# Rotated queries and retention keys turned by VectorE in squares of 32 and by DMAs, in place of TensorE transposes

## What is computed

```python
for l in range(DEPTH_2):
    h = rms_norm(x, pre_norm_g[l])
    (rq, rk, rv, rg, dq, dk, dv, dg, lx, lg) = jnp.split(jnp.einsum('bsd,de->bse', h, w_in[l]), split_idx, axis=-1)
    ro = retention(rq, rk, rv, positions)             # 6 heads of 128, rotated q and k, decayed causal scores
    do = diff_attention(dq, dk, dv, positions, lam)   # 4 heads, 2 x 64 rotated q and k, two softmaxes
    ... # lru_out from lx, lg
    y = jnp.einsum('bse,ed->bsd', mixed, w_out[l])
    x = x + rms_norm(y, post_norm_g[l])
```

## Time and profile before

| what | value |
|---|---|
| median of 3 executions | 2645.58 us (2645.3 to 2647.14) |
| profiled execution | 2647.02 us, span 2645.2 us |
| PE busy | 2556.9 us, 97% |
| PEld busy | 2147.6 us, 81% |
| DVE busy | 1699.3 us, 64% |
| ACT busy | 1282.6 us, 48% |
| POOL busy | 63.3 us, 2% |
| mean granted TensorE clock | 0.994 of full |
| DMA queue of SP (q1), share of 16 engines | 64.6% |

### The profile page before, as it was taken

The page is one execution under the profiler, slowest core; times in us unless marked ns, Lnnn a source line. Parts: engine busy times, 40 slices in busy tenths (PEclk is TensorE's granted clock), DMA queues, the critical chain, the costliest instruction groups (busy, mean ns, idle before and its releaser), DMA issues.

```text
span 2645.2 us, 33987 instructions
## 1 busy us (share of the span) xinstructions
PE 2556.9 (97%) x12327; PEld 2147.6 (81%) x12327; DVE 1699.3 (64%) x2194; ACT 1282.6 (48%) x1824; POOL 63.3 (2%) x102
## 2 busy tenths in 40 slices
PE   3889999999999999999999999999999999999999
PEld 3888887888887887788888888888888887988887
DVE  5887776776676755566655545565666655676664
ACT  3345455444555444544443444455755545565553
POOL 0000000000000000000000000000000100010000
PEclk9999999999999999999999999999999999999999
DMA  9984665888675765687756666556665465665564
GB/s 363 340 262 152 184 207 183 286 308 269 205 251 192 237 205 180 192 281 252 269 190 192 191 191 190 183 186 182 182 188 175 136 216 148 187 187 176 150 200 135
DMA packets 279921, 555.73 MB, mean 210 GB/s; under 512 B 24287, under 2 KB 45101, under 8 KB 279117
## 3 DMA queue, kind: packets, MB, share of 16 engines
q1 hardware_dynamic: 274048, 541.79, 64.6%
q0 software_dynamic: 3040, 8.69, 1.0%
q10 hardware_dynamic: 2668, 3.09, 0.3%
HBM read 549.83 MB, written 2.10 MB: 209 GB/s over the span
## 4 chain that ended last, share of the span: by engine, by line
PE 90%; DVE 4%; ACT 2%; issue 1%; DMA 1%; SPq 0%; POOL 0%; DVEq 0%; ACTq 0%
PE gp L830 83%; PE tp L830 5%; PE tp L833 2%; DMA raw_first<-in_ada_w_dram 1%; DVE wlo L1884 1%; ACT whi L1270 1%; DVE acc L1890 1%; DVE xs L1884 0%; ACT hraw L1270 0%; SPq L813 0%; DVE stat L2208 0%; ACT sx L1270 0%; DVE sx L1884 0%; DVE yd L1884 0%; ACT h L1270 0%
## 5 line engine op out<-in xcount | busy, mean ns | idle before, releaser
L1884 DVE TENSOR_TENSOR wlo<-raw,whi 128x1024 fp32r<-128x1024 f32 (+1 forms) x830 | 986.1, 1197 | 699.7 <-ACT whi L1270 697.1
L830 PE MATMUL gp<-whi,h 128*128 128x512 f32 (+1 forms) x4352 | 1373.2, 389 | 11.5 <-DVE h L1884 5.5
L1270 ACT ACTIVATE whi<-raw 128x1024 fp32r<-128x1024 f32 (+1 forms) x830 | 851.5, 1037 | 666.6 <-PE gp L830 537.3
L830 PEld LDWEIGHTS gp<-whi,h 128*128 128x128 f32 x4352 | 816.4, 188 | 171.5 <-issue 19.6
L830 PE MATMUL gp<-wlo,h 128*128 128x512 f32 (+1 forms) x2176 | 835.6, 384 | 0.0
L830 PEld LDWEIGHTS gp<-wlo,h 128*128 128x128 f32 x2176 | 410.4, 189 | 72.8 <-issue 1.7
L1890 DVE SCALAR_TENSOR_TENSOR acc<-raw,cact,acc 128x1024 f32<-128x1024 f32 x149 | 190.6, 1279 | 7.7 <-DMA raw<-in_ada_w_dram 7.0
L830 PE MATMUL gp<-whi,ah 128*128 128x512 f32 x352 | 138.0, 392 | 0.0
L830 PE MATMUL gp<-whi,al 128*128 128x512 f32 x352 | 137.1, 390 | 0.0
L830 PE MATMUL gp<-wlo,ah 128*128 128x512 f32 x352 | 137.0, 389 | 0.0
L830 PE MATMUL gp<-h,whi 128*128 128x256 f32 (+1 forms) x528 | 107.2, 300 | 20.7 <-ACT whi L1270 10.7
(11 more groups left out here) (331 smaller groups left out, 2594.2 us busy)
## 6 DMA issues: line engine op xcount, KB each, us to landing
raw<-in_w_in_dram SPq DMA_DIRECT2D x310, 512.0 KB, 4.3
raw<-in_ffn_w_in_dram SPq DMA_DIRECT2D x176, 512.0 KB, 4.5
raw<-in_ada_w_dram SPq DMA_DIRECT2D x158, 512.0 KB, 5.0
raw<-in_w_out_dram SPq DMA_DIRECT2D x96, 512.0 KB, 4.4
raw<-in_ffn_w_down_dram SPq DMA_DIRECT2D x88, 512.0 KB, 4.4
raw<-in_w_in_dram SPq DMA_DIRECT2D x64, 384.0 KB, 3.5
raw_first<-in_ada_w_dram SPq DMA_DIRECT2D x34, 512.0 KB, 7.5
raw<-in_gla_wo_dram SPq DMA_DIRECT2D x32, 512.0 KB, 5.7
```

The costliest lines, as they stand in the source:

```text
L830: return e.matmul(o, l, r, start=start, stop=stop)
L1270: return e.activation(o, i, f, **kw)
L1884: return e.tensor_tensor(o, a, b, op)
```

## The change

The planner gives dq and rqk, in place of the two steps `rp_T`, one step `rp_t`, the one after the second rotation step (so one unit later), with no PSUM bank. dk keeps its way over PE. `rp_t` on DVE turns each 128 tokens in squares of 32 with one transpose of 128 x 512, from `st` to a new buffer STT, written in steps of four values; before, it waits until the last job's DMAs have landed. `rp_t` on POOL waits for both transposes and issues 16 DMAs inside SBUF, each of 32 partitions x 2 x 512 bytes, that carry the squares to their partitions, into DQB or RQB: four tiles interleaved, so a tile's values stand 16 bytes apart. `df_S` reads its stationary side (the query) so, `rt_S` both sides. PE waits for the DMAs (`d_rp`) where it waited for ACT's copies, and ACT waits for `rp_turned` before it fills `st` again.

```diff
     if kind in ("dq", "dk", "rqk"):
         l, j = args
-        return [step(("rp_r", (kind, l, j, 0), 0), need=[("lru", l)]), step(("rp_r", (kind, l, j, 1), 0)), idle, idle] + \
-            [step(("rp_T", (kind, l, j, k), 1)) for k in (0, 2)] + [idle]
+        steps = [step(("rp_r", (kind, l, j, 0), 0), need=[("lru", l)]), step(("rp_r", (kind, l, j, 1), 0))]
+        if kind == "dk":
+            return steps + [idle, idle] + [step(("rp_T", (kind, l, j, k), 1)) for k in (0, 2)] + [idle]
+        return steps + [step(("rp_t", (kind, l, j), 0))] + [idle] * 4
...
+    STT, DQB, RQB = w2("stt", 0, [2, 512]), w2("dqb", 32, [1, S, 4]), w2("rqb", 56.25, [3, S, 4])
...
+    def quadrants(b, n, t0, t1):
+
+        return b[:, n // 4, P * t0:P * t1, n % 4]
...
         def roped(kind, l, j):
+            if kind != "dk":
+                w.wait_ge(d_rp, at("rp", kind, l, j))
+                return
...
-            mm(bk[:, 0:S], RQK[:, 6 + h, 0:P], RQK[:, h, :], True, True)
-            mm(bk[:, S:384], RQK[:, 6 + h, P:S], RQK[:, h, P:S], True, True).then_inc(tp_full[u.b], 1)
+            first, second = (quadrants(RQB, 6 + h, t, t + 1) for t in range(2))
+            mm(bk[:, 0:S], first, quadrants(RQB, h, 0, 2), True, True)
+            mm(bk[:, S:384], second, quadrants(RQB, h, 1, 2), True, True).then_inc(tp_full[u.b], 1)
...
-                last = mm(bk[:, c0:c0 + n], DQT[rows, h, t * P:(t + 1) * P], DKT[c if h < 2 else 0][rows, h, 0:n], True, True)
+                last = mm(bk[:, c0:c0 + n], quadrants(DQB[rows], h, t, t + 1), DKT[c if h < 2 else 0][rows, h, 0:n], True, True)
...
+                    if of[0] in ("dq", "rqk"):
+                        w.wait_ge(rp_turned, at("turned", *of))
...
+        def rp_t(us, kind, l, j):
+            w.wait_ge(rope_done, at("rope", kind, l, j))
+            w.wait_ge(d_rp, 256 * rp_n[0])
+            rp_n[0] += 1
+            for t in range(2):
+                e.transpose(STT[:, t, :].rearrange("p (q i b) -> p q b i", q=4, b=4),
+                            ST2[job_of[kind, l, j]["st2"]][:, t, :].rearrange("p (b q i) -> p q b i", q=4, b=4)).then_inc(rp_turned, 1)
+            note(rp_turned, "turned", kind, l, j)
...
+        def rp_t(us, kind, l, j):
+            to = (DQB if kind == "dq" else RQB)[:, j, :, :].rearrange("p (t a i) b -> p t a (i b)", t=2, a=4)
+            w.wait_ge(rp_turned, at("turned", kind, l, j))
+            for a in range(4):
+                for q in range(4):
+                    e.dma_start(to[32 * q:32 * q + 32, :, a, :], STT[32 * a:32 * a + 32, :, P * q:P * q + P]).then_inc(d_rp, 16)
+            note(d_rp, "rp", kind, l, j)
```

More of the change, by code:

```diff
@@ L593, in program @@
     d_xg = sem("d_xg")
+    rp_turned, d_rp = sem("rp_turned"), sem("d_rp")
     hi_done, lo_done, mm_done, mm_half, ada_dve = (sem(n) for n in ("hi_done", "lo_done", "mm_done", "mm_half", "ada_dve"))
@@ L2385, in rp_r @@
             note(rope_done, "rope", kind, l, j)
+        rp_n = [0]
+        def rp_t(us, kind, l, j):
[6 more added lines that the diff above has]
+            note(rp_turned, "turned", kind, l, j)
         def rt_S(us, l, h):
@@ L2588, in dve_program @@
                      f_rn=f_rn, f_sc=f_sc, f_hi=f_hi, fx_T=fx_T, hx_T=hx_T, le_T=le_T, lf_rn=lf_rn, lf_g=lf_g, ls_rn=ls_rn, ls_rs=ls_rs, lx_T=lx_T, lx_conv=lx_conv, lru_e=lru_e, lru_a=lru_a,
-                     lru_b=lru_b, lg_T=lg_T, rp_r=rp_r, rt_S=rt_S, rt_n=rt_n, rt_s=rt_s, rt_M=rt_M, rt_T=rt_T, df_S=df_S, df_W=df_W, df_V=df_V, df_X=df_X,
+                     lru_b=lru_b, lg_T=lg_T, rp_r=rp_r, rp_t=rp_t, rt_S=rt_S, rt_n=rt_n, rt_s=rt_s, rt_M=rt_M, rt_T=rt_T, df_S=df_S, df_W=df_W, df_V=df_V, df_X=df_X,
                      le_rn=le_rn, le_y=le_y, le_add=le_add, evac=evac)
@@ L2690, in evac @@
                 e.dma_start(XR[j % 2][:, :, :], x_cols[:, :, j, :]).then_inc(d_xr[j % 2], 16)
-        parts = dict(prep=prep, x_ss=x_ss, gla_loads=gla_loads, gk_krt=gk_krt, rp_T=rp_T, gla_av=gla_av, f_rn=f_rn, f_gfb=f_gfb, lf_rn=lf_rn, ls_rn=ls_rn, lru_b=lru_b, rt_n=rt_n, df_V=df_V,
+        parts = dict(prep=prep, x_ss=x_ss, gla_loads=gla_loads, gk_krt=gk_krt, rp_T=rp_T, rp_t=rp_t, gla_av=gla_av, f_rn=f_rn, f_gfb=f_gfb, lf_rn=lf_rn, ls_rn=ls_rn, lru_b=lru_b, rt_n=rt_n, df_V=df_V,
                      rt_gp=rt_gp, le_rn=le_rn, evac=evac)
```

## The result

The changed kernel takes 2681.8 us (median of 4, 2680.3 to 2684.0) beside 2645.9 for the kernel before on the same chip: ratio 1.0136, interval 1.0122 to 1.0150. It is slower by 36 us. The forecast was slower by 16, with a range up to 2677, so the sign and the mechanism of the waits are right, and the size is wrong by a factor of two. The profiled execution has a span of 2680.4 us, 35.2 more than before.

What follows compares the result with a forecast made beforehand. PE was taken as the bound; a layer summed -3.7 + 0.9 + 3.5 + 4.9 + 3.0 = +8.6 us, two layers +17.2, added to the median 2645.6: 2662.8, said as 2662, range 2650 to 2677.

Steps and rivals of the forecast that it cites:

- what is bound, and where it waits: PE, busy 97% of the span, sets the pace; time leaving its queue shortens the run, its waits lengthen it.
- All four bursts: POOL's sixteen DMA issues for dq and rqk 0 to 2: +0.9, hidden, +3.5 and +4.9 us a layer.
- POOL's issue: Each DMA issue on POOL's queue takes 0.52 us, so 8.3 us for sixteen; ends 0.50 and 0.74.
- the stepped reads: Score products df_S and rt_S reading in steps of 16 bytes: taken to cost nothing.
- the dear case: Rival: the stepped reads cost their second pass, forecast + 7.8 = 2670 us; chance 0.2.
- The upper bound of 7.8 + 3: Most the stepped reads could cost: 7.8 us with rt_S's moving side at half speed, 3 more for df_S's weight loads.
- first reading: Cacheline note: two hits on a 16-byte line needed for full bandwidth; by it the sum is some 8 us higher.
- 3.5: PE's wait at df_X of head 2, behind rqk 1's burst delaying POOL's power: +3.5 us a layer.
- 4.9: PE's wait at the first rt_S for rqk 2's last DMA landing: +4.9 us a layer.
- a turn: Two VectorE transposes of 128x512 for each job: 1.3 us, bounds 0.7 and 2.6.
- the dq stage: DVE's turn delays the wlo for dv 3 and dv 4, so PE waits: +0.9 us a layer; dq's data lands in time.
- the clock: TensorE's clock falls to half at both waits, 1.5 us left behind each: +3.0 us a layer.

Runs made afterwards that it cites:

- The run with the later rqk 1: Changed kernel with the turn of rqk 1 (transposes and DMAs) two units later, behind df_V of head 2: 2672.0 us, ratio 1.0103.
- the run with four DMAs: Changed kernel with four DMAs of 128 partitions for a job in place of sixteen of 32, same bytes, no turning across quadrants: 2660.8 us, ratio 1.0061.
- the run with both moved: Changed kernel with the turn of rqk 1 two units later and the retention three units later: 2652.0 us, ratio 1.0030.
- with free steps and the two moves: Changed kernel with rqk 1's turn two units later, the retention three later, and two tiles interleaved (steps of 8 bytes): 2641.0 us, ratio 0.9987.

## Why the prediction was wrong, step by step

**Right: what is bound, and where it waits.** All four bursts behave as read off the order. dq: POOL issues from 1934.81 for 8.43 us, and nothing waits for the data. rqk 0: hidden. rqk 1 and 2: PE waits at df_X of head 2 and at the first rt_S, in both layers. The run with the later rqk 1 takes away the first, the run with four DMAs the first and most of the second, the run with both moved both. POOL's issue was forecast at 0.52 us and is 0.53.

**Wrong: the stepped reads.** This is the step that failed. I took nothing, by the argument that a float32 value has twice the time of a gemm value, and gave the dear case 0.2. It costs 13.5 us alone (ratio 1.0051) and 9 in the changed kernel, where 14 us more of PE work stand partly in the place of waits. The upper bound of 7.8 + 3 was too low as well. A pair of rt_S, with both sides stepping, takes 2.1 times as long, not 2 (2.79 for 1.31), 8.9 us in all; no run steps only its moving side. A df_S, of which only the weight load steps (0.327 us for 0.188), loses 0.26 to 0.40, 5.3 us in all. Its bound was also read beside the wrong row: the 0.33 us of the earlier trace rows are the products of rt_S, and those of df_S take a median of 0.374. The Trainium skill (SBUF — State Buffer, Door 1: The DMA port swizzle, its note on cachelines) was right in its first reading, that two hits on a line of 16 bytes are needed: steps of 8 are as good as free (1.0001), steps of 16 are not (1.0051). Its remark that four float32 are the stride that is free is contradicted by these runs, in which a step of four float32 is the dear one. That a stated rule spoke against the change, and that no row spoke for it, should have moved the chance above a half.

**Mis-sized: the waits.** 3.5 was 4.4 and 4.9 was 6.6 in layer 0. Three terms: a turn is 2.04 us for 1.3, since a transpose that writes in steps of 16 bytes takes 1.08 (flat it takes 0.69, just what the slope of the earlier trace rows gave); POOL starts 0.3 us behind the turn, where 0.1 was assumed; and the last landing takes 3.1 for 2.5. In layer 1 the wait on dg is 6.0: POOL stood still for 1.78 us behind the third issue of the burst, for which its profile shows no reason.

**Mis-sized: the dq stage.** +0.9 was +1.75 (0.65 and the 1.1 that were to go), mostly by the longer turn (0.7).

**Over-sized: the clock.** 3.0 a layer was 1.5 in layer 0 (and 2.8 in layer 1, 4.73 - 2.75 and 6.27 - 5.46). Most of the second fall lies under stepped products, and these take as long at either clock: the first pair of rt_S takes 2.74 us to the next product both at half clock (2084.64 to 2087.38) and, with PE kept busy, at full (2084.22 to 2086.96).

**The range.** It was made of single errors. The stepped reads (+14) and the longer waits (+6, and +2 at the dq stage) have separate causes and came together, so a sum of the two belonged inside it.

## What to carry over

Count the issues on a queue that also computes: sixteen of 0.53 us ahead of a 0.7 us operation that two engines wait for cost more than the PE transposes that they replaced, and moving them two units in the order gave 9 us back. Interleave at most so far that two values fall into each 16 bytes; in steps of 16 bytes the same float32 copy, transpose, weight load or pair of products cost 1.6 to 2.1 times what it costs without steps. And a change that loses through two causes is judged only when each is taken away alone: with free steps and the two moves the same idea ends 0.13% ahead of the kernel before. The moves must then be tried without the change as well, and here they weren't: more than half of that 0.13% may be theirs.

## What the hardware showed unexpectedly

- Steps of 16 bytes cost on all three engines that were tried: ACT's write of 128x512 1.09 us for 0.60, DVE's transpose 1.08 for 0.69, PE's weight load 0.311 for 0.190, a pair of rt_S 2.79 for 1.31. Steps of 8 bytes: 0.63, 0.405 for 128x256, 0.194, 1.37.
- A pair of rt_S in steps of 16 bytes takes 2.74 us to the next product at 1.2 and at 2.4 GHz (2.73 and 2.74 in layer 1); contiguous ones take 2.56 at the lower clock (2081.35 to 2083.91 in the run with reads without steps) and 1.31 in the chain at the higher.
- The stretch between the layers takes 2.3 us more where the clock falls in it, in kernels that differ only elsewhere. That is close to the size of gain that was at stake.
- POOL's pauses come at the same issue each time. They stand in layer 1 behind the third issue of rqk 1's burst (1.73 to 1.78 us) in all six profiles with sixteen DMAs of 512-byte pieces, and in dq's burst (0.48 and 1.57) in both with pieces of 256 bytes. Neither layer 0 nor the run with four DMAs has one.
- What stays open: the cause of these pauses, and why the clock falls in the stretch between the layers in some kernels and not in others.
